# The second model's mixer in another order: a query copy ahead of two weight splits, three value projections a step later, two half output blocks behind the transposes

## What is computed

```python
hn = rms_norm(h, attn_norm)
c_q, c_kv, k_rope, dq, dk, dv, sq, sk, sv = split(hn @ w_in)
# diff: 4 heads, two softmaxes each, subtracted with lambda
y_b = rms_norm((softmax(dq1 dk1) - lam * softmax(dq2 dk2)) @ dv)
# swa: 6 query heads on 2 key heads, a window of 128, a sink
y_c = softmax_with_sink(sq sk) @ sv
# mla: 6 heads; queries, keys and values are made from small latents
q = rms_norm(c_q) @ w_qb          # 6 x (64 + 32 rotary)
k_nope, v = split(rms_norm(c_kv) @ w_kvb)
y_a = softmax([q_nope, rot(q_rope)] . [k_nope, rot(k_rope)]) @ v
h = h + concat(y_a, y_b, y_c) @ w_out
```

## Time and profile before

| what | us |
|---|---|
| median of 3 runs (range) | 1344.52 (1343.17 to 1349.12) |
| the profiled execution, its own time | 1343.38 |
| its span | 1341.5 |
| PE / PEld busy | 1295.4 (97%) / 1150.3 (86%) |
| DVE / ACT / POOL busy | 988.4 (74%) / 734.3 (55%) / 121.5 (9%) |

### The profile page before, as it was taken

How to read it: one execution, slowest core, us unless ns; L and a number is a source line. 1 busy time by engine, 2 the same in 40 slices (tenths; PEclk the granted TensorE clock), 3 DMA queues, 4 the chain that set the end, 5 groups by cost and what they waited for, 6 DMA issues and landing times.

```text
span 1341.5 us, 24506 instructions
## 1 busy us (share of the span) xinstructions
PE 1295.4 (97%) x8567; PEld 1150.3 (86%) x8567; DVE 988.4 (74%) x1848; ACT 734.3 (55%) x1330; POOL 121.5 (9%) x189
## 2 busy tenths in 40 slices
PE   6999998889999999999999999999999889999997
PEld 6999988679999999999989899999988757888886
DVE  6878777858877779777776759777775555877774
ACT  5555555556555556555555646555564544655553
POOL 3321002010000000000011202000013400000000
PEclk9999999989999999999999999999999989999999
DMA  9999656415766656666659537666648301666660
GB/s 256 269 267 264 188 174 161 129 48 163 222 186 187 190 166 189 189 188 188 187 164 239 178 115 229 197 187 188 189 113 217 108 13 47 199 187 186 188 180 32
DMA packets 295469, 233.59 MB, mean 174 GB/s; under 512 B 13164, under 2 KB 270516, under 8 KB 295408
## 3 DMA queue, kind: packets, MB, share of 16 engines
q1 hardware_dynamic: 288432, 214.07, 54.3%
q0 software_dynamic: 6688, 18.60, 5.5%
q10 hardware_dynamic: 288, 0.10, 0.0%
HBM read 229.79 MB, written 7.55 MB: 177 GB/s over the span
## 4 chain that ended last, share of the span: by engine, by line
PE 89%; DVE 5%; ACT 4%; issue 1%; DMA 0%; POOL 0%; ACTq 0%; POOLq 0%; DVEq 0%
PE gu L1962 42%; PE y L1974 16%; PE y L2050 4%; PE gu L2338 4%; PE y L2016 2%; PE gu L1941 2%; PE gu L2163 2%; PE y L1997 2%; PE gu L1997 2%; PE gu L2132 2%; DVE sb_w_lo L1304 1%; ACT sb_prob L1004 1%; PE gu L2422 1%; PE y L2376 1%; PE gu L2191 1%
## 5 line engine op out<-in xcount | busy, mean ns | idle before, releaser
L1962 PE MATMUL gu<-sb_act_t,sb_w_hi 128*128 128x512 f32 x1680 | 587.7, 394 | 0.0
L1304 DVE TENSOR_TENSOR sb_w_lo<-sb_w_raw,sb_w_hi 128x1024 fp32r<-128x1024 f32 (+1 forms) x405 | 500.0, 1239 | 104.0 <-ACT sb_w_hi L865 98.5
L865 ACT ACTIVATE sb_w_hi<-sb_w_raw 128x1024 fp32r<-128x1024 f32 (+1 forms) x405 | 423.9, 1052 | 70.8 <-PE y L1974 29.6
L1962 PE MATMUL gu<-sb_act_t,sb_w_lo 128*128 128x256 f32 x1680 | 434.6, 279 | 0.0
L1962 PEld LDWEIGHTS gu<-sb_act_t,sb_w_hi 128*128 128x128 f32 x1680 | 307.4, 188 | 55.3
L1962 PEld LDWEIGHTS gu<-sb_act_t,sb_w_lo 128*128 128x128 f32 x1680 | 316.1, 188 | 14.9
L1974 PE MATMUL y<-sb_hid_t,sb_w_hi 128*128 128x256 f32 x1216 | 218.5, 280 | 0.0
L927 ACT ACTIVATE sb_work<-gu 128x256 f32<-128x256 f32 x220 | 83.8, 382 | 238.3 <-PE gu L1962 230.2
L1974 PEld LDWEIGHTS y<-sb_hid_t,sb_w_hi 128*128 128x128 f32 x1216 | 190.7, 188 | 3.7 <-issue 0.3
L1974 PE MATMUL y<-sb_hid_t,sb_w_lo 128*128 128x256 f32 x608 | 170.2, 280 | 0.0
L1427 DVE TENSOR_TENSOR sb_work<-gu,sb_work 128x256 f32<-128x256 f32 x220 | 92.6, 423 | 96.1 <-ACT sb_work L927 96.1
(11 more groups left out here) (333 smaller groups left out, 1672.1 us busy)
## 6 DMA issues: line engine op xcount, KB each, us to landing
sb_w_raw<-in_ffn_w_gate SPq DMA_DIRECT2D x88, 512.0 KB, 3.9
sb_w_raw<-in_ffn_w_up SPq DMA_DIRECT2D x88, 512.0 KB, 3.9
sb_w_raw<-in_ffn_w_down SPq DMA_DIRECT2D x88, 512.0 KB, 3.7
sb_w_raw<-in_odd_w_qkv SPq DMA_DIRECT2D x24, 512.0 KB, 4.8
sb_w_raw<-in_w_gate SPq DMA_DIRECT2D x22, 512.0 KB, 3.9
sb_w_raw<-in_w_up SPq DMA_DIRECT2D x22, 512.0 KB, 3.9
sb_w_raw<-in_w_down SPq DMA_DIRECT2D x22, 512.0 KB, 3.7
sb_w_raw<-in_even_w_in SPq DMA_DIRECT2D x12, 512.0 KB, 3.7
```

Of the source, the lines that this page charges most:

```text
L865: nc.scalar.activation(w_hi[:, slot, 0:w], w_raw[:, slot, 0:w], ACT.Copy).then_inc(hi_done, 1)
L1304: nc.vector.tensor_tensor(w_lo[:, slot, 0:w], w_raw[:, slot, 0:w], w_hi[:, slot, 0:w].bitcast(F32), ALU.subtract).then_inc(lo_done, 1)
L1962: ins = nc.tensor.matmul(gu[:, b, w, 0:width], part[:, s, cols], act_t[:, k, 0:width], start=(k == 0 and i == 0), stop=(k == KT - 1 and i ...
```

## The change

Nothing is added or removed; five calls stand at other places.

- VectorE, step j = 2: `chunk_out(2)` is ahead of `split(13)` instead of behind it.
- VectorE, step j = 3: `chunk_out(3)` moves from behind the scores and normalisation of pair 4 to ahead of them; `split(15)` moves from ahead of `chunk_out(4)` to behind it.
- TensorE and ScalarE: latents 10, 11 and 12 and their copies move from the end of step 5 to step 6, on TensorE behind the values of pair 5 and ahead of the scores of pair 7, on ScalarE behind `finish_unit` of pair 5 and ahead of `copy_probs` of pair 6.
- TensorE, steps 8 and 9: the half output blocks 4 and 5 move from ahead of the scores (in step 9, of the transposes) to behind the transposes, directly ahead of the values of the same pair.

```diff
@@ ScalarE, second_mix
-                    for step in {4: (0, 1, 2), 5: (7, 8)}.get(j, ()):
+                    for step in {4: (0, 1, 2), 5: (7, 8), 6: (10, 11, 12)}.get(j, ()):
                         latent_copy(step)
...
-                    for step in {4: (3, 5), 5: (9, 10, 11, 12)}.get(j, ()):
+                    for step in {4: (3, 5), 5: (9,)}.get(j, ()):
                         latent_copy(step)
@@ VectorE, second_mix
                     if j < 4:
                         split(8 + 2 * j)
+                    if j == 3:
+                        chunk_out(3, n0)
                     if j == 5:
                         turn_rot(1)
                     if j + 1 < len(SECOND_PAIRS):
...
-                    if j == 3:
-                        chunk_out(3, n0)
-                    if j < 4:
-                        split(9 + 2 * j)
                     if j == 2:
                         chunk_out(2, n0)
                     if j == 3:
                         chunk_out(4, n0)
+                    if j < 4:
+                        split(9 + 2 * j)
@@ TensorE, second_mix
-                    for step in {4: (0, 1, 2), 5: (6, 7, 8)}.get(j, ()):
+                    for step in {4: (0, 1, 2), 5: (6, 7, 8), 6: (10, 11, 12)}.get(j, ()):
                         latent(step)
-                    if j >= 7:
-                        half_block(n0 + IN2_BLOCKS, "second", {7: 2, 8: 4, 9: 5}[j], (0, 1))
+                    if j == 7:
+                        half_block(n0 + IN2_BLOCKS, "second", 2, (0, 1))
...
-                    for step in {4: (3, 4, 5), 5: (9, 10, 11, 12)}.get(j, ()):
+                    for step in {4: (3, 4, 5), 5: (9,)}.get(j, ()):
                         latent(step)
...
-                    if j == 7:
-                        half_block(n0 + IN2_BLOCKS, "second", 3, (0, 1))
+                    if j >= 7:
+                        half_block(n0 + IN2_BLOCKS, "second", j - 4, (0, 1))
```

## The result

| | before | after |
|---|---|---|
| median of 5 runs each, us (range) | 1345.39 (1343.17 to 1349.40) | 1334.09 (1331.32 to 1336.76) |
| profiled execution, us (its span) | 1343.38 (1341.5) | 1331.32 (1329.5) |
| mean granted clock of that execution | 0.990 | 0.996 |

The ratio after to before is 0.9912, with a 95% interval of 0.9885 to 0.9939: 11.3 us, or 8 to 15. The forecast of 1335.9 us lies 1.8 us above the measured median. Its sum, 8.6 us, lies at the lower end of the interval for what was gained.

The account below looks back on a forecast made before the run. TensorE, busy 97% of the span, was taken as the bound, with 9.5 us of idle in the changed stretch. Idle of 6.1 us plus 2.45 us of clock made 8.6 us, giving a median of 1335.9 us, range 1331.5 to 1341.5.

Parts of the forecast that it names:

- A: Ahead of chunk 3: TensorE's 2.94 us wait shrinks by 1.14 us, 1.8 stays; the low clock behind costs 1.4.
- B: Ahead of latents 0 and 1: 1.8 us of idle shrinks by 1.1, 0.7 stays; low clock behind costs 1.4.
- D: Pairs 8 and 9: two 1.27 us waits for `copy_probs` filled by half blocks 4 and 5; net -2.0 us.
- C: Latents 10 to 12: 2.31 us wait used for pair 5's values, -1.9 us; low clock behind worth 1.05.
- The values' time leaves the chain: -1.9: At latents 10 to 12: pair 5's values run inside the 2.31 us wait instead of behind the latents, saving 1.9 us.
- I take A and C as gained (2.45) and B as still lost.: Full clock returns at chunk 3 and latents 11 and 12, 2.45 us; not near pair 4's transposes, amid light work.
- the idle time at 221 to 224 us: Before the changed stretch: 2.7 us of idle cited as not followed by a fall of the clock.
- The rule of the Trainium skill: Warns only of idle gaps longer than the three here; by it, shortening them gives no clock back.
- All three places: Rival: clock comes back at chunk 3, latents 0 and 1, and latents 10 to 12; 10.0 us, 1334.5 us; chance 0.22.
- The clock doesn't come back: Rival: clock stays low or falls elsewhere, only idle goes; 6.1 us, 1338.4 us; none or only one place back 0.20.
- Caught up: Rival: latent 12, pair 9's transposes or pair 6's values wait longer; gain 2 to 4 us, about 1341.5; chance 0.09.
- The lasting low stretch: Rival: from latent 10 on the clock stays low; about +4 us, 1348.5 us; chance 0.04.

Follow-up runs that it names:

- B alone: Kernel before with only `chunk_out(3)` moved ahead of pair 4's scores and `split(15)` behind `chunk_out(4)`: 1342.81 us, ratio 0.9979.
- A alone: Kernel before with only `chunk_out(2)` moved ahead of `split(13)`: 1343.37 us, ratio 0.9983.
- the four single-part kernels: Kernel before with only the change's part at A, B, C or D: 1343.37, 1342.81, 1340.35 and 1342.65 us.
- the fill: Kernel before with the key transposes ahead of chunk 3 issued six times instead of once: 1345.12 us in one run.
- the two further ones: Changed kernel with `chunk_out(2)` and `chunk_out(4)` ahead of normalisation: 1332.22 us; that plus latents 10 to 12 spread, step 9's copy ahead of exponentials: 1330.27 us.

## Why the prediction was right, and where it was not

**The waits moved as it said.** 1.8 us at A, none ahead of L2302, 0.7 ahead of L2198 (0.8 measured), under 0.5 for L1074 (0.2), `copy_probs` ahead of pair 5's values 0.7 (0.5), and a new wait inside pair 9's transposes of 0.5 (0.3). The terms for A and B, -1.14 and -1.1, were measured as -1.15 and -1.14. D's -2.0 was measured as -2.00, but 2.54 us of waits gone and 0.3 new would make -2.2; 0.2 us went elsewhere in that piece, so the exact agreement is luck.

**C: the sum was right, its two terms mis-sized.** "The values' time leaves the chain: -1.9" took the values' duration from rows that ran partly at half speed: 1.86 us, where they take 1.38 after the change. The end at 1093.2 us in the same paragraph does not fit 1.9 us either: `copy_probs` ends at 1091.02, and latent 10 needs 0.9. At full speed the idle part is 1.3 us, and the fall there costs 1.6 and not 1.05. Together 2.9, where 2.95 was forecast, but only in executions in which the clock fell at C before: three of the five with the old order there.

**The clock: the step that failed.** "I take A and C as gained (2.45) and B as still lost." It was the other way round. B's 1.46 came back and A's 1.55 did not. As the two prices are alike, the sum in the stretch came out at 8.65 against 8.6 all the same, and that is luck. The reason given was that B keeps its idle place amid the lightest work and A has dense work behind it. It did not hold: A's fall was there in every profile with 1.79 us of idle time, with the dense work behind it. What the runs show is that at A, B and C falls got rare once little idle time was left (at A not yet at 1.79 us):

| place | idle time | profiles in which the clock fell |
|---|---|---|
| A | 2.94 us | 4 of 4 |
| A | 1.79 | 4 of 4 |
| A | 0.3 or none | 0 of 5 |
| B | 1.0 and 0.8 (once 0.8 and 0.6), with 0.66 of transposes between | 5 of 5 |
| B | 0.76 to 0.9 | 1 of 8 |
| C | 2.31 | 3 of 5 |
| C | 0.5 and less | 0 of 8 |
| D | twice 1.27 | 1 of 5 |

B's profiles with one 0.8 us place left include the kernel with B alone. From one place to another the length does not decide: 2.31 us at C brought no fall in two profiles of five, while 1.79 at A always did. Nor does it decide at one and the same place. The prediction took the idle time at 221 to 224 us as one that no fall follows. It is there in all 13 profiles, 2.68 or 2.69 us long, ahead of L2440, and the clock fell at it in seven and stayed at 1.00 in six. First the changed kernel, then the one with A alone, with the stretch behind the idle time of each:

```profile
223.78 0.47 PE L2440 MATMUL gu<-sb_act_t,sb_w_hi 128*128 128x256 f32 x2 [2.69 <-ACT sb_work L1194]
...
227.70 0.47 PE L2440 MATMUL gu<-sb_act_t,sb_w_hi 128*128 128x256 f32 x2 [2.68 <-ACT sb_work L1194]
```

```profile
223.80:227.20 3.40, 3.40 (x26) 3.12 (x26) 2.97 (x5) 1.54 (x3) 0.87 (x1) 1.00 0.81 164
228.80:232.20 3.40, 3.40 (x18) 3.40 (x17) 1.88 (x3) 0.19 (x1) 0.00 (x0) 0.50 0.93 174
```

So one profile could not tell which idle places bring a fall, and the prediction's comparison with this place and with D rested on one. What decides besides the length is open: D, for one, has dense half blocks ahead of its idle time, but no run changed that alone. The rule of the Trainium skill that the prediction set against the trace ("TensorE: Matmul & The Clock Gate", section "Why this matters for your kernels") fares no better: all these gaps are shorter than those it warns of (A's 2.94 us only just), and filling A's or removing it did give the clock back, as did shortening B's in seven profiles of eight.

**The size of the clock's share.** The forecast had 6.1 us of idle time, 2.45 us of clock and a total of 8.6. Piece by piece the idle part was 5.6 us (1.15, 1.14, 1.3 and 2.0), and the fit's 6.1 ± 1.3 agrees with both. The fit leaves about 5.3 of 11.4 us to what goes with the clock. The one profile of before showed each fall once, 3.4 us long. Other executions have 6.8 us at A or B (in two of the four single-part kernels) and now and then a fall at D. Taken over the profiles with the old order at each place, and priced as measured (about 1.5 us for a fall of 3.4 us, 0.9 to 1.0 more for one of 6.8), the falls come to an estimated 3.3 us more than the one that stays at A. The rest, some 2 us, would lie outside the stretch. There the six profiles of the kernel before, of the four parts and of the fill come to s3 at 1051.7 us on average (1048.0 to 1054.6), the seven of the changed kernel and the two further ones at 1048.6 (1045.9 to 1050.3). Of these 3.1 us 2.4 arise between 59 and 105 us, where the wait for L1448 lies, with the fall behind it. The instructions there are the same, the two ranges overlap, and no run was made to test it. Whether that is chance or something that the later part does to the earlier one is open, and so is why VectorE comes late there.

**The rivals.** "All three places" falls with A's fall, in each of three profiles of the changed kernel. "The clock doesn't come back" falls with B. "Caught up" had the right place to look at: latents 11 and 12 and pair 9's transposes do wait, but for 0.15 and 0.3 us only. The lasting low stretch did not come in any profile; the longest was 6.8 us. That the shift stays whole behind the mixer is borne out: from v9 to the end of the span it took 213.65 us before and 213.66 after.

## What to carry to other kernels

When one engine is the bound, price an idle place on it by its own length and by what the clock does behind it (here 5.6 us of idle time, and 3.1 us of half speed between the two profiles), with durations from rows at full clock, and read from several executions whether the clock falls there. Compare traces piece by piece between the same instructions, since one execution's total can point the wrong way. What another engine waits for belongs ahead of work that nobody waits for, and a filler belongs behind the step that starts the next chain, or it lengthens that chain, as latent 12 did.

## What the runs showed of the hardware

- TensorE's clock fell to its lower level (granted clock 0.50) at idle times as short as 1.79 us in four profiles of four, and once at an idle place of 0.88 us (the 6.8 us shown above). Yet at one idle place of 2.68 us in the first model, the same in every kernel, it fell in seven of 13 profiles only.
- A low stretch lasted 3.4 or 6.8 us in this mixer, whatever came next. One of 3.4 us cost 1.46 to 1.6 us, one of 6.8 us about 2.4. In the first model one of 3.4 us, from 247.3 us on in the kernel before, cost nothing that the profile shows.
- The same program has its falls at different places from one execution to the next. Most of the spread of the runs of the kernel before, 12.7 us (1338.11 to 1350.77) or nearly 1%, goes with their clock, and part of that spread can be idle time, such as the wait of up to 3.6 us near 81 us.
- Small float32 transposes in an idle place kept the clock up, in the one profile that tried it, as well as removing the idle time did in four.
